# Adaptive modulation in four column strips, split over two places; memory keys and values moved to the start

## The chip, the core and the metric

The program is one kernel on one core of a Trainium2 chip. The core has five engines with a queue of instructions each: TensorE (PE; its weight loads are PEld), VectorE (DVE), ScalarE (ACT), GpSimd (POOL) and SyncE (SP, which here only issues transfers). An engine works strictly through its own queue; between engines, order is kept by semaphores that an instruction raises and another waits for. The metric is the device time of one execution in microseconds (us).

## The reference, cut to what matters

The whole computation is a hybrid mixer block, a feed-forward block and two attention or recurrent layers over 1024 tokens of width 1024. The change touches three small pieces of it: the modulation of the first block (a vector of 1024 times a matrix of 1024 x 6144, giving six vectors), the first norm that uses two of them, and the keys and values of a memory of 256 rows, which only the second block reads.

```
c_act = jax.nn.silu(c)
mod = c_act @ ada_w[l] + ada_b[l]
sh1, sc1, gt1, sh2, sc2, gt2 = [m[:, None, :] for m in jnp.split(mod, 6, axis=-1)]
h = rms_norm(x, pre1_w[l]) * (1.0 + sc1) + sh1
y = hybrid_mixer(h, w_in[l], ...)
x = x + (1.0 + gt1) * rms_norm(y, post1_w[l])
h = rms_norm(x, pre2_w[l]) * (1.0 + sc2) + sh2
...
mem_kv = (mem @ w_mem_kv[layer]).reshape(b, MEM_LEN, 2, N_MEM_HEADS, HEAD_DIM)
```

So the mixer needs `sh1` and `sc1` (a third of the matrix) before its first product; `gt1`, `sh2`, `sc2`, `gt2` are needed only when the mixer is done.

## The kernel before, in words

**Blocks.** The program is a row of blocks; all engines meet at a barrier between two of them. In a block, `side_by_side` takes several parts, and each part yields a planned time before each step on each engine; the steps are merged by these planned times, and that alone sets the order of an engine's queue. The planned times are not waits. An instruction that waits for a semaphore holds up all that stands behind it on its engine.

**Weights.** All products with large weights run in two-part precision: a weight slot is 128 x 1024 numbers (512 KB). SP fetches it into one of two raw buffers (`raw_w`), ACT rounds it (`round_slot`, L269), POOL subtracts to get the rest (`rest_of_slot`, L278, which raises `w_split`), and both halves go to a ring of four slots. PE then makes three products per weight tile (hi x hi, hi x lo, lo x hi; `three`, L286). A raw buffer is free for the next transfer when POOL is done with it; a place in the ring is free when PE is done with its slot.

**The front block** (L1212) does four things. The modulation (L967) streams 48 slots of 512 KB of `ada_w` in plain f32 through PE: the vector, repeated over 128 columns, is the stationary operand, and each slot is two products of 128 x 128 by 128 x 512 into one PSUM bank. All 128 rows of the result are the same; DVE picks the diagonal (L993, L997) for each group of four slots. `squares` loads x in four quarters and sums squares; `statistic` makes the mean and root (L819 to L851); `normed` scales x on DVE (L1074), rounds it with the shift added on ACT (L1086) and takes the rest on DVE (L1078), which gives `h_hi` and `h_lo`, the moving operand of the mixer. The memory part (L1108 to L1198) lies in x's buffer, so it starts when the norm is done; its two layers of keys and values use weight slots 0 to 7 and leave through DRAM.

**The three mixer blocks** behind it multiply h with the weight stream. The second of them (L1728) uses PSUM banks 0 to 3 for other work; the third (L1828) runs twelve products of 8 k-tiles by 1024 tokens (gate, queries, S5 inputs; banks 4 to 7 only), with a convolution on DVE beside them, and then eight products of 4 k-tiles that merge. A block that waits for the keys and values to be in DRAM (`finish(kv_written)`, L915) stands between the first and the second.

## Time and profile before

| what | value |
|---|---|
| time, median of 3 runs | 3321.97 us |
| the three runs | 3309.07, 3321.97, 3329.38 us |
| profiled execution, span | 3327.0 us |
| PE busy | 3077.8 us, 93% of the span |
| DVE, ACT, POOL busy | 39%, 29%, 24% |
| read from DRAM, written | 207.10 MB, 51.99 MB; 78 GB/s over the span |
| memory traffic in the first 105 us | 34.35 MB, mean 327 GB/s |
| first product of the mixer starts at | 139.10 us |

The profiled execution's time is known only as its span from the first to the last instruction, 3327.0 us, which lies among the three runs (0.15% above their median). In the profile, PE is busy nearly throughout, so time is lost or won where PE waits, and where it does work that could be shorter.
### The profile page before, as it was taken

To read this page: it belongs to the slowest core of one execution; us is meant where nothing else is said; L and a number is where in the kernel's file an instruction comes from. 1 tells how busy PE (TensorE), PEld (TensorE's weight loads), DVE (VectorE), ACT (ScalarE), POOL (GpSimd) and SP (SyncE) were. 2 spreads that over 40 slices of the span, in tenths; PEclk is the share of its full clock that TensorE was granted. 3 is DMA by queue.
4 is the path that set the end of the run, shared out by engine and by line. 5 is a ranking of instruction groups with operands and counts; after the bars stand their busy time and mean duration, and the time that the engine had idled before them with its cause. 6 is when DMAs were issued, how large, how long until landed. Compare 5 with 4: busy or idle time off the path is not lost. (4 is left out here: it accounts for less than half of the span.)

```text
span 3327.0 us, 33614 instructions
## 1 busy us (share of the span) xinstructions
PE 3077.8 (93%) x14024; PEld 2305.5 (69%) x14024; DVE 1302.5 (39%) x1342; ACT 977.6 (29%) x1264; POOL 809.4 (24%) x380
## 2 busy tenths in 40 slices
PE   8899999999989898999999999998789998899886
PEld 3677777877766576688888787776466666667565
DVE  5153111333425443300000245331656663528555
ACT  3232222212134123311111354332233441247312
POOL 1223112215332122322222345322021211223100
PEclk9999999999989899899999999998789999999897
DMA  9411111252132342111111233312100001111201
GB/s 355 140 52 58 57 51 57 108 177 77 64 131 92 107 172 72 55 44 50 44 44 50 75 112 123 112 51 86 57 19 15 20 14 70 64 70 38 92 13 51
DMA packets 76485, 261.01 MB, mean 78 GB/s; under 512 B 8048, under 2 KB 12384, under 8 KB 75328
## 3 DMA queue, kind: packets, MB, share of 16 engines
q1 hardware_dynamic: 76352, 259.13, 22.1%
q8 instruction: 97, 1.59, 0.2%
q14 instruction: 36, 0.29, 0.0%
HBM read 207.10 MB, written 51.99 MB: 78 GB/s over the span
## 5 line engine op out<-in xcount | busy, mean ns | idle before, releaser
L278 POOL TENSOR_TENSOR w_lo_sb<-raw_w_sb,w_hi_sb 128x1024 fp32r<-128x1024 f32 x231 | 579.5, 2509 | 2003.1 <-ACT w_hi_sb L269 2002.9
L269 ACT ACTIVATE w_hi_sb<-raw_w_sb 128x1024 fp32r<-128x1024 f32 x231 | 243.1, 1052 | 418.1 <-PE ps L286 369.0
L286 PE MATMUL ps<-merged_parts_hi_sb,w_hi_sb 128*128 128x512 f32 x832 | 336.0, 404 | 16.4 <-PEq L533 7.7
L286 PE MATMUL ps<-merged_parts_lo_sb,w_hi_sb 128*128 128x512 f32 x832 | 332.3, 399 | 0.0
L286 PE MATMUL ps<-h_hi_sb,w_hi_sb 128*128 128x512 f32 x720 | 296.4, 412 | 14.7 <-PEq L907 11.1
L286 PE MATMUL ps<-h_lo_sb,w_hi_sb 128*128 128x512 f32 x720 | 288.4, 401 | 0.0
L286 PE MATMUL ps<-merged_parts_hi_sb,w_lo_sb 128*128 128x512 f32 x832 | 274.1, 398 | 0.0
L286 PE MATMUL ps<-h_hi_sb,w_lo_sb 128*128 128x512 f32 x720 | 245.1, 400 | 0.0
L286 PE MATMUL ps<-z_lo,w_hi_sb 128*128 128x512 f32 x512 | 205.8, 402 | 0.0
L286 PEld LDWEIGHTS ps<-merged_parts_hi_sb,w_hi_sb 128*128 128x128 f32 x832 | 158.4, 190 | 61.9 <-issue 13.8
L2768 DVE TENSOR_TENSOR ffn_hidden_sb<-ffn_hidden_sb,ps 128x1024 f32 x20 | 24.4, 1221 | 426.0 <-PE ps L286 426.0
L286 PEld LDWEIGHTS ps<-merged_parts_hi_sb,w_lo_sb 128*128 128x128 f32 x832 | 158.3, 190 | 39.7
L286 PEld LDWEIGHTS ps<-merged_parts_lo_sb,w_hi_sb 128*128 128x128 f32 x832 | 158.5, 191 | 37.2 <-issue 0.5
L286 PE MATMUL ps<-z_hi,w_hi_sb 128*128 128x512 f32 x384 | 162.7, 424 | 15.9 <-POOL z_lo L3517 5.9
L286 PEld LDWEIGHTS ps<-h_hi_sb,w_hi_sb 128*128 128x128 f32 x720 | 137.9, 191 | 53.1 <-issue 18.5
L286 PEld LDWEIGHTS ps<-h_hi_sb,w_lo_sb 128*128 128x128 f32 x720 | 137.6, 191 | 34.0
L286 PEld LDWEIGHTS ps<-h_lo_sb,w_hi_sb 128*128 128x128 f32 x720 | 138.2, 192 | 32.1 <-issue 1.0
L286 PE MATMUL ps<-hid_hi_sb,w_hi_sb 128*128 128x512 f32 x352 | 141.2, 401 | 7.7 <-DVE hid_lo_sb L2863 7.7
L286 PE MATMUL ps<-hid_lo_sb,w_hi_sb 128*128 128x512 f32 x352 | 140.2, 398 | 0.0
L286 PE MATMUL ps<-hid_hi_sb,w_lo_sb 128*128 128x512 f32 x352 | 139.1, 395 | 0.0
L3225 PE MATMUL ps<-qh_sb,kh_sb 97*128 97x512 f32 (+3 forms) x288 | 125.3, 517 | 13.1 <-DMA qh_sb<-att_rows 10.5
L286 PE MATMUL ps<-z_hi,w_lo_sb 128*128 128x512 f32 x384 | 133.9, 403 | 0.0
(571 smaller groups left out, 5571.9 us busy)
## 6 DMA issues: line engine op xcount, KB each, us to landing
raw_w_sb<-in_w SPq DMA_DIRECT2D x231, 512.0 KB, 3.2
ada_w_sb<-in_ada SPq DMA_DIRECT2D x48, 512.0 KB, 7.2
inbox_sb<-gates_out SPq DMA_DIRECT2D x24, 512.0 KB, 4.1
gates_out<-outbox_sb SPq DMA_DIRECT2D x16, 512.0 KB, 2.6
inbox_sb<-sums_out SPq DMA_DIRECT2D x16, 512.0 KB, 4.7
spilled_sum<-x_sb SPq DMA_DIRECT2D x32, 256.0 KB, 2.0
x_sb<-spilled_sum SPq DMA_DIRECT2D x2, 4096.0 KB, 13.5
x_sb<-in_x SPq DMA_DIRECT2D x4, 1024.0 KB, 10.9
```

The source lines that it names most:

```text
L269: nc.scalar.activation(w_hi[:, n % RING].rearrange("p t m -> p (t m)"), raw_w[:, n % RAW], ACT.Copy).then_inc(w_rounded.sem, 1)
L278: nc.gpsimd.tensor_tensor(w_lo[:, n % RING].rearrange("p t m -> p (t m)"), raw_w[:, n % RAW], flat_hi, ALU.subtract).then_inc(w_split.sem, 1)
L286: mm = nc.tensor.matmul(o, wt, xs, start=start and part == 0 and xs is x_hi, stop=stop and part == 1)
L2768: return nc.vector.tensor_tensor(late[:, tile], late[:, tile], src, ALU.mult)
L3225: mm = nc.tensor.matmul(ps[:, 4 + n % 2, 0:hi - lo], k_of(u)[0:dq + 1, s * P:(s + 1) * P], q_of(u)[0:dq + 1, lo:hi], start=True, stop=not ...
```

## The change

1. The modulation product is cut into four column strips of 32: the stationary operand is the vector repeated over 32 columns, and the four strips of the array take four different pieces of 128 columns of the slot. The slots are laid out anew on the host side to suit. DVE picks from 128 x 128 instead of 128 x 512.
2. Only the first 16 of the 48 slots are done in the front (ring of 6 buffers instead of 8). The other 32 go into the third mixer block (`late_modulation`), one slot at each 4.2 us of planned time, with two buffers.
3. The memory keys and values come at the start of the front: their input lies where `h_lo` will be, so the first writes of `h_lo` wait until all eight steps are done (`kv_t`, 8). The raw weight transfers 2 to 13 are issued among the modulation's.
4. In the norm, half of the `h_lo` work goes from DVE to POOL, at the price of one more ACT instruction for these tiles.
5. The wait for keys and values in DRAM moves from a block of its own into SP's queue at the end of the front block.

```diff
-ADA_RING = 8
+ADA_RING = 6
 ADA_SLOTS = 48
+ADA_EARLY = 16
...
+        wide_scope = ctx.enter_context(ExitStack())
+        act0_wide = sb_in(wide_scope, "ada_silu", [P, DT, 32], high=True)
+        own_row = sb_in(wide_scope, "ada_own_row", [P, 32], high=True)
...
+        def modulate(n, slot, bank, count):
+
+            for k in range(2):
+                for s in range(4):
+                    mm = nc.tensor.matmul(ps[strip_of(s), bank, 0:P], act0_wide[:, 2 * (n % 4) + k],
+                                          slot[:, k, s * P:(s + 1) * P], start=(n % 4 == 0 and k == 0),
+                                          stop=(n % 4 == 3 and k == 1), tile_position=(0, 32 * s))
+            mm.then_inc(count.sem, 1)
+
+        def pick_group(g, pick, bank, picked, link):
+
+            nc.vector.tensor_tensor(pick, ps[:, bank, 0:P].rearrange("p (j i) -> p j i", i=32),
+                                    own_row[:].unsqueeze(1).broadcast_to([P, 4, 32]), ALU.mult).then_inc(picked[0].sem, 1)
+            link.eng.wait_ge(picked[0].sem, picked[1])
+            link(nc.vector.tensor_reduce(mod[:, 4 * g:4 * g + 4], pick, AX.X, ALU.add))
...
-            S = lambda n: 8.0 + 1.9 * n
-            X = lambda i: S(2 + 5 * i)
+            S = lambda n: 12.0 + 2.2 * n
+            X = lambda i: 4.0 + 8.0 * i
+            K = lambda n: 15.0 + 3.2 * n
+            N0 = S(ADA_EARLY) + 2.0
...
-                    for n in range(ADA_SLOTS):
+                    for n in range(ADA_EARLY):
                         yield S(n)
...
-                        for k in range(2):
-                            mm = nc.tensor.matmul(ps[:, n // 4 % 2], act0_wide[:, 2 * (n % 4) + k],
-                                                  ada_w[:, n % ADA_RING, k], start=(n % 4 == 0 and k == 0),
-                                                  stop=(n % 4 == 3 and k == 1))
-                        mm.then_inc(pe_done.sem, 1)
+                        modulate(n, ada_w[:, n % ADA_RING], n // 4 % 2, ada_done)
...
+            split_at = lambda n: 10.5 + 2.6 * n if n < RING else K(n - RING) + 4.6
+
             def first_slots():
-                at = lambda n: S(8 + 4 * (n - RAW)) if n >= RAW else -1.0 + n
-
                 def on_sp(sp):
-                    for n in range(RING + RAW):
-                        yield at(n)
+                    for n in range(RING + 8 + RAW):
+                        yield -3.0 + 0.1 * n if n < RAW else split_at(n - RAW) + 2.6
                         if n >= RAW:
                             sp.wait_ge(w_split.sem, n - RAW + 1)
                         sp.dma_start(raw_w[:, n % RAW], a["w"][n]).then_inc(w_full[n % RAW].sem, 16)
...
                 def on_dve(dve, link):
                     for t in range(10):
-                        yield A + 1.7 * t
+                        yield A + 1.2 * t
...
-                        if t >= 2:
+                        if t >= 2 and t % 2 == 0:
                             dve.wait_ge(hi_s.sem, n - 1)
+                            if n == 2:
+                                dve.wait_ge(kv_t.sem, 8)
                             nc.vector.scalar_tensor_tensor(H[1][:, t - 2, cols], x0[:, t - 2, cols], mod[:, t - 2:t - 1],
...
+                        if t % 2 == 0:
+                            nc.scalar.activation(H[0][:, t, cols], x0[:, t, cols], ACT.Identity, bias=mod[:, t:t + 1]
+                                                 ).then_inc(hi_s.sem, 1)
+                        else:
+                            nc.scalar.activation(x0[:, t, cols], x0[:, t, cols], ACT.Identity, bias=mod[:, t:t + 1]
+                                                 ).then_inc(biased_s.sem, 1)
+                            act.wait_ge(biased_s.sem, n // 2 + 1)
+                            nc.scalar.activation(H[0][:, t, cols], x0[:, t, cols], ACT.Copy).then_inc(hi_s.sem, 1)
+
+                def on_pool(pool, link):
+                    for t in range(1, 8, 2):
...
+                        pool.wait_ge(hi_s.sem, n + 1)
+                        nc.gpsimd.tensor_tensor(H[1][:, t, cols], x0[:, t, cols], H[0][:, t, cols].bitcast(F32),
+                                                ALU.subtract).then_inc(lo_pool_s.sem, 1)
...
-            memT = sb_over("mem_in", [P, DT, MEM], F32, x0_at)
...
+            memT = sb_over("mem_in", [P, DT, MEM], F32, h_lo_at)
+            MT = (sb_over("mem_parts_hi", [P, DT, MEM], F32R, h_lo_at + 8 * T),
+                  sb_over("mem_parts_lo", [P, DT, MEM], F32R, h_lo_at + 16 * T))
+            km = [sb_in(scope, f"mem_k{layer}", [65, MEM_HEADS, MEM]) for layer in range(2)]
+            vm = [sb_in(scope, f"mem_v{layer}", [P, MEM // P, MEM_HEADS, P]) for layer in range(2)]
...
             def memory_keys():
                 def on_sp(sp):
-                    yield after_norm
-                    sp.wait_ge(lo_s.sem, 16)
+                    yield -2.5
                     sp.dma_start(memT[:], a["mem"]).then_inc(mem_s.sem, 16)
...
+                    yield N0 + 20.0
+                    sp.wait_ge(kv_written.sem, 64)
 
                 def on_pe(pe):
...
-                            yield at + m * step
+                            yield K(n)
...
+        def late_modulation(scope, at, pace):
+
+            slots = sb_in(scope, "ada_late", [P, 2, 2, HALF])
...
+            n_late = ADA_SLOTS - ADA_EARLY
+            L = lambda n: at + pace * n
+
+            def on_sp(sp):
+                for n in range(n_late):
+                    yield L(n - 2) + 0.6
+                    if n >= 2:
+                        sp.wait_ge(*done.at(n - 1))
+                    sp.dma_start(slots[:, n % 2].rearrange("p k m -> p (k m)"), a["ada"][ADA_EARLY + n]
+                                 ).then_inc(full[n % 2].sem, 16)
+
+            def on_pe(pe):
+                for n in range(n_late):
+                    yield L(n)
+                    if n % 4 == 0 and n >= 8:
+                        pe.wait_ge(*picked.at(n // 4 - 1))
+                    pe.wait_ge(*full[n % 2].at(16 * (n // 2 + 1)))
+                    modulate(n, slots[:, n % 2], n // 4 % 2, done)
+
+            def on_dve(dve, link):
+                for g in range(n_late // 4):
+                    yield L(4 * g + 3) + 1.2
+                    dve.wait_ge(*done.at(4 * g + 4))
+                    pick_group(g + ADA_EARLY // 4, pick[:], g % 2, (picked, picked.n + g + 1), link)
...
-            finish(kv_written)
-            kv_scope.close()
             finish(rows_written)
...
-            side_by_side(gate, gating(), queries, convolution(), inputs, Part(None, ready), merging)
+            late = late_modulation(s2, 8.0, 4.2)
+            side_by_side(gate, gating(), queries, convolution(), inputs, Part(None, ready), merging, late)
...
+def _by_strip(slots):
+
+    n = slots.shape[0]
+    return np.ascontiguousarray(slots.reshape(n, P, 2, 4, 4, 32).transpose(0, 1, 2, 4, 3, 5)).reshape(n, P, SLOT * P)
```

**SP in the front block.** `ada_w` are the modulation's slots, `raw_w` the weight slots, `x` the quarters of the input; `pe_done` is raised by a modulation slot in the kernel before, `ada_done` in the changed one. Before, from its first wait on:

```order
L955 DMA ada_w_sb_60<-in_ada 128x1024 [waits pe_done]
L1037 DMA x_sb_57<-in_x 128x4x512
L955 DMA ada_w_sb_60<-in_ada 128x1024 [waits pe_done] x5
L1037 DMA x_sb_57<-in_x 128x4x512
L955 DMA ada_w_sb_60<-in_ada 128x1024 [waits pe_done]
L1016 DMA raw_w_sb_49<-in_w 128x1024 [waits w_split]
```

And in the changed kernel, from its first wait on:

```order
L984 DMA ada_w_sb_62<-in_ada 128x1024 [waits ada_done]
L1029 DMA raw_w_sb_49<-in_w 128x1024 [waits w_split]
L984 DMA ada_w_sb_62<-in_ada 128x1024 [waits ada_done]
L1029 DMA raw_w_sb_49<-in_w 128x1024 [waits w_split]
L984 DMA ada_w_sb_62<-in_ada 128x1024 [waits ada_done]
L1029 DMA raw_w_sb_49<-in_w 128x1024 [waits w_split]
L984 DMA ada_w_sb_62<-in_ada 128x1024 [waits ada_done]
L1050 DMA x_sb_59<-in_x 128x4x512
L1029 DMA raw_w_sb_49<-in_w 128x1024 [waits w_split]
```

Where there was a weight transfer after every fourth or so modulation slot, the two now take turns, and the third quarter of x stands behind three weight transfers that wait for POOL.

**PE in the third mixer block**, in the middle of one of its products (`h_hi`, `h_lo` times weights). Before:

```order
L286 MATMUL ps<-h_hi_sb_58,w_hi_sb_50 128x512
L286 MATMUL ps<-h_lo_sb_59,w_hi_sb_50 128x512
L286 MATMUL ps<-h_hi_sb_58,w_hi_sb_50 128x512
L286 MATMUL ps<-h_lo_sb_59,w_hi_sb_50 128x512
L286 MATMUL ps<-h_hi_sb_58,w_lo_sb_51 128x512 x2
```

Changed, with one late slot of the modulation between two k-tiles (the semaphore shown as `mem_loaded` is a used one, taken over for the late slots' landing):

```order
L287 MATMUL ps<-h_hi_sb_60,w_hi_sb_50 128x512
L287 MATMUL ps<-h_lo_sb_61,w_hi_sb_50 128x512
L287 MATMUL ps<-h_hi_sb_60,w_lo_sb_51 128x512 x2
L939 MATMUL ps<-ada_late_sb_3361,ada_silu_sb_57 32x128 [waits mem_loaded]
L939 MATMUL ps<-ada_late_sb_3361,ada_silu_sb_57 32x128 x7
L287 MATMUL ps<-h_hi_sb_60,w_hi_sb_50 128x512
L287 MATMUL ps<-h_lo_sb_61,w_hi_sb_50 128x512
```

There are 32 such places, each of eight short products, each with its own wait for a transfer.

**SP in the third mixer block**, of the changed kernel: the late slots' transfers stand among waits for POOL (`w_split`) and for ACT (`ml_silu`). Their wait (shown as `mem_lo`, also a used semaphore) is for the late slot two before.

```order
L1249 DMA ada_late_sb_3361<-in_ada 128x1024 [waits mem_lo] x3
L589 DMA raw_w_sb_49<-in_w 128x1024 [waits w_split]
L1249 DMA ada_late_sb_3361<-in_ada 128x1024 [waits mem_lo]
L1851 DMA ml_qk_out<-conv_box_sb_3343 128x1024 [waits ml_silu]
L1249 DMA ada_late_sb_3361<-in_ada 128x1024 [waits mem_lo]
```

In the kernel before, the same stretch holds the `raw_w` and `ml_qk_out` transfers alone.

## Rows read from the trace of the kernel before

**Rows 1.** Stretches: us, busy us (records) by engine, granted clock, DMA share, GB/s
```profile
0.00:20.00 20.00, 12.72 (x23) 5.57 (x24) 2.07 (x3) 3.61 (x4) 4.86 (x6) 1.00 0.92 352
20.00:60.00 40.00, 35.84 (x84) 16.34 (x82) 22.14 (x34) 15.63 (x24) 4.70 (x2) 0.91 1.03 398
...
105.00:128.00 23.00, 23.00 (x193) 22.73 (x191) 3.02 (x11) 9.39 (x15) 12.07 (x6) 1.00 0.38 131
128.00:139.10 11.10, 0.01 (x1) 0.03 (x1) 0.88 (x4) 2.11 (x2) 6.92 (x3) 0.71 0.69 226
533.00:712.00 179.00, 178.68 (x761) 143.32 (x759) 49.42 (x32) 38.90 (x35) 41.45 (x16) 0.99 0.34 115
```

**Rows 2.** Timeline of PE in the front: start, length, engine, line, operation, count
```profile
69.01 36.21 PE L967 MATMUL ps<-ada_w_sb,ada_silu_sb 128*128 128x512 f32 x84
104.66 0.68 PE L286 MATMUL ps<-mem_parts_hi_sb,w_hi_sb 128*128 128x256 f32 x1
...
127.72 0.28 PE L286 MATMUL ps<-w_hi_sb,mem_parts_lo 128*128 128x256 f32 x1
139.10 0.76 PE L286 MATMUL ps<-h_hi_sb,w_hi_sb 128*128 128x512 f32 x1 [11.10 <-PEq L907]
```

**Rows 3.** Timeline of POOL, last row of the front
```profile
134.72 2.34 POOL L278 TENSOR_TENSOR w_lo_sb<-raw_w_sb,w_hi_sb 128x1024 fp32r<-128x1024 f32 x1 [1.42 <-ACT w_hi_sb L269]
```

**Rows 4.** Timeline of SP and ACT: first quarter of x issued, and first used
```profile
11.43 0.43 SPq L1037 DMA_DIRECT2D x_sb<-in_x  x1
...
22.71 0.63 ACT L1049 ACTIVATE norm_total_sb<-x_sb 128x512 f32<-128x512 f32 x1 [9.34 <-DMA x_sb<-in_x]
```

**Rows 5.** Transfers of the page, whole span: KB each, median us to landing
```profile
raw_w_sb<-in_w SPq DMA_DIRECT2D x231, 512.0 KB, 3.2
```

**Rows 6.** Groups by line, page: busy us, mean ns of one
```profile
L278 POOL TENSOR_TENSOR w_lo_sb<-raw_w_sb,w_hi_sb 128x1024 fp32r<-128x1024 f32 x231 | 579.5, 2509 | 2003.1 <-ACT w_hi_sb L269 2002.9
L269 ACT ACTIVATE w_hi_sb<-raw_w_sb 128x1024 fp32r<-128x1024 f32 x231 | 243.1, 1052 | 418.1 <-PE ps L286 369.0
```

**Rows 7.** Timeline of DVE in the first norm
```profile
76.34 0.74 DVE L1078 SCALAR_TENSOR_TENSOR h_lo_sb<-x_sb,mod_sb,h_hi_sb 128x512 fp32r<-128x512 f32 x1
77.01 0.74 DVE L1074 SCALAR_TENSOR_TENSOR x_sb<-x_sb,fold_sb,ps 128x512 f32<-128x512 f32 x1
77.67 0.74 DVE L1078 SCALAR_TENSOR_TENSOR h_lo_sb<-x_sb,mod_sb,h_hi_sb 128x512 fp32r<-128x512 f32 x1
```

**Rows 8.** Timeline of ACT: two with a bias back to back, two without
```profile
73.16 1.38 ACT L1086 ACTIVATE h_hi_sb<-x_sb,mod_sb 128x512 fp32r<-128x512 f32 x2 [2.43 <-DVE x_sb L1074]
...
23.25 1.13 ACT L1049 ACTIVATE norm_sq_sb<-x_sb 128x512 f32<-128x512 f32 x2
```

**Rows 9.** Groups of POOL by shape: half-width subtractions elsewhere
```profile
L3517 POOL TENSOR_TENSOR z_lo<-x_sb,z_hi 128x512 fp32r<-128x512 f32 x8 | 10.8, 1346 | 42.7 <-ACT z_hi L3511 42.7
```

**Rows 10.** Timeline of PE: column strips of 32 inside a stream of two-part products
```profile
809.83 0.39 PE L286 MATMUL ps<-h_lo_sb,w_hi_sb 128*128 128x512 f32 x1
810.06 0.40 PE L286 MATMUL ps<-h_hi_sb,w_lo_sb 128*128 128x512 f32 x1
810.39 3.70 PE L1944 MATMUL ps<-s_state_sb,s_c_powers_sb 128*32 128x128 f32 x128
814.02 0.50 PE L286 MATMUL ps<-h_hi_sb,w_hi_sb 128*128 128x512 f32 x1
814.35 0.40 PE L286 MATMUL ps<-h_lo_sb,w_hi_sb 128*128 128x512 f32 x1
```

**Rows 11.** Timeline of PE: sixteen records in strips, twice as wide
```profile
787.44 1.07 PE L1926 MATMUL ps<-s_c_powers_sb,s_bbar_sb 128*32 128x256 f32 x16 [1.12 <-POOL act_sb L2005]
788.45 0.50 PE L286 MATMUL ps<-h_hi_sb,w_hi_sb 128*128 128x512 f32 x1
```

**Rows 12.** Waits of PE from 128 to 800 us: total, times, longest
```profile
PE ps L286 <- PEq L915: 2.9, 1, 2.9
...
PE ps L286 <- PEq L1268: 2.5, 1, 2.5
```

**Rows 13.** Groups of DVE by line, 533 to 712 us
```profile
L1792 DVE SCALAR_TENSOR_TENSOR conv_box_sb<-ml_raw_sb,vec_sb,conv_box_sb 128x1024 f32<-128x1024 f32 x12 | 23.5, 1960 | 0.4
```

**Rows 14.** Timeline of SP in the third mixer block: transfers in regular steps
```profile
597.50 0.33 SPq L1808 DMA_DIRECT2D ml_qk_out<-conv_box_sb  x1
605.20 0.33 SPq L588 DMA_DIRECT2D raw_w_sb<-in_w  x1
608.69 0.33 SPq L1808 DMA_DIRECT2D ml_qk_out<-conv_box_sb  x1
```

154 lines of the change are left out of this document (69 added, 85 removed).

## The prediction

> **What bounds the kernel now.** I read the stretches first. From 0 to 60 us two things are full at once: PE, nearly all of it modulation, and the memory traffic at about 400 GB/s; the granted clock is near 1. From 105 to 128 us PE works on keys and values while memory is at 131 GB/s, and from 128 to 139 us PE does nothing. From 533 to 712 us, in the third mixer block, PE is busy 178.68 of 179 us [rows 1]. So the front leaves PE's main work, the two-part products, unstarted for 139.10 us [rows 2], and everything behind it is bound by PE: what is put into the third block is paid in full, what is taken from the front is gained in full as long as nothing else there takes its place.
>
> The timeline of PE then gives the prices. 84 modulation records take 36.21 us, 0.43 us each, four to a slot: 1.72 us, against 512 KB / 0.405 MB/us = 1.3 us of transfer. Keys and values are 192 products from 104.66 to 128.0 us, 2.9 us for each of eight weight slots [rows 2]. The idle 11 us are the weight pipeline: POOL's last split ends at 137.06 [rows 3], the barrier follows, and PE starts 2.0 us later [rows 2].
>
> **The front, step by step.** Removed from PE: 32 slots x 1.72 = 55 us. The remaining 16 slots cost 0.78 us each as strips (next part): 12 us. Keys and values stay 8 x 2.9 = 23 us but lie beside the transfers. PE therefore needs some 35 us at full clock, POOL 12 splits x 2.5 = 30 us [rows 6], so neither alone is the bound.
>
> Transfers: they land in the order of issue. The first quarter of x was issued at 11.43 with 7.6 MB up to its end, and was used at 22.71 [rows 4]: that is 4 us + 7.6 MB / 0.405. The changed order has, up to the last of the 16 slots, 26 transfers of 0.52 MB, x with 4.2, the memory rows with 1.05, constants 0.75, stored keys and values 0.8: 20.4 MB, so 54 us if SP never had to hold. It does hold. There are two raw buffers, and SP issues raw slot n+2 only after split n; landing 3.2 us at least [rows 5], rounding 1.05, split 2.5 [rows 6]: 6.8 us for each pair, plus 1.3 us for every other slot that lies ahead of it in the transfers. Walking the new order of SP, ACT, POOL and PE with these durations I get: split 0 at 14 us (ACT first waits for the memory rows), raw 3 issued at 21, raw 4 at 30, the third quarter of x landed at 37, the fourth at 50, raw 9 landed at 57, modulation slot 15 at 59. PE in its strict order does the last value step until 62, then the sums of the fourth quarter, then the last strips until 67; picking, bias and fold on DVE end at 69. The bounds of this point: 59, if the holds cost nothing (54 and the last strips and picks), and 88, if TensorE runs the whole front at 1.2 GHz, so that each key step takes 5.7 us and PE's own queue is the chain.
>
> The norm follows whole, because the scaling of both halves stands behind the second root on DVE. DVE steps are 0.66 us apart [rows 7]. Of each two tiles DVE now does three operations (1.98 us); ACT does a biased rounding and a biased write (two back to back take 1.38) and a copy (0.57, half of 1.13) [rows 8], with a semaphore between, some 2.04 us. Eight such pairs: 16.3 us; the first scaling 0.7; behind the last rounding one POOL subtraction of half width, 1.35 us [rows 9]. Together 18.4 us, so the block ends at 87.5 to 88 and the mixer's first product starts at 90 (2.0 us of barrier as before). **Gain 49 us**; with the bounds of the fold, 60 and 30.
>
> **The price of a late slot.** The trace holds this very instruction elsewhere: 128 x 32 stationary, 128 x 128 moving, four strips in turn [rows 10]. From the product at 810.06 to the one at 814.35 pass 4.29 us; two ordinary steps of 0.23 are in it, so 128 records with their change of mode cost 3.82. Sixteen records of twice the width take 1.01 us up to the next product [rows 11], without the 0.10 us lag on entry (810.39 - 810.06 - 0.23) and the 0.10 after the first product (814.35 - 814.02 - 0.23). With g for a group of four records and o for entry and exit: 32 g + o = 3.82 and 8 g + o - 0.20 = 1.01, so g = 0.109 us and o = 0.34. The four strips do overlap. A slot is sixteen records: 4 x 0.109 + 0.34 = 0.78 us, and **32 late slots cost 25 us**, all on PE's path. Bounds: 14 us (no o), and 67 us (records one after another, 16 x 0.109 + 0.34).
>
> The Trainium skill has two rules against this part. "TensorEngine Tiling (Array Packing)", Key Properties, says that changing the tiling mode drains TensorE; o is what the trace shows of it. "TensorE: Matmul & The Clock Gate", in the section on 56 ns, gives an issue bound of about 62 ns per matmul when the decoding is not done in hardware; by it a slot would be 16 x 62 ns + 0.34 = 1.33 us and the late part 43 us. The trace disagrees, 27 ns per record [rows 10].
>
> **The rest of the third block.** Late transfers are 16.8 MB in about 200 us and fit beside 115 GB/s [rows 1]. A slot's transfer is issued when the slot two before is done, some 10 us ahead of its use, and lands in 3.2 us [rows 5]; SP's regular steps there show it not holding long for others [rows 14]. The picks add eight pairs of small operations to DVE, which is busy 49 of 179 us [rows 1], with its convolution at 2 us an operation [rows 13]. The banks used (0, 1) are free. I cost all this at nothing; if the cover of 10 us went, each slot would cost PE up to its landing. The removed barrier block: three meetings took 2.9 us of PE and two took 2.5 [rows 12]; I take 1 us.
>
> **The sum.** -49 - 1 + 25 = -25 us: 3302 against the profiled 3327.0, and 3297 against the median 3322, which lies 5 us below the profiled span. About 1%, 33 us, is what a measurement here can tell from no change.
>
> **Rivals.**
> - *TensorE cold in the front* (12%). For it: its clock fell in the stretches with idle PE (0.71 from 128 to 139 us [rows 1]), and the new front has waits for splits of up to 6 us between its pieces. Against: the old front with its gaps stayed at 0.91 [rows 1]. Fold at 88, product at 109: -30 - 1 + 25, time 3316.
> - *A shorter front* (10%). Transfers hold SP less than my walk says; fold near 60: -59 - 1 + 25, time 3287.
> - *Issue-bound strips* (3%). If short bursts cost by the record and not by the group of four, the dearest step that a row shows is 1.01 / 16 = 0.063 us [rows 11]; a slot is then 16 x 0.063 + 0.34 = 1.35 us and the late part 43 us, time 3315. Against: the long burst [rows 10]. The Trainium skill's issue bound, above, is this rival.
> - *Strips that do not overlap here* (3%), the change not doing what it says: 67 us instead of 25, and some 10 us more in the front, time 3349. Rows 10 speak plainly against.
> - *Starved late slots, slower than before* (4%). SP's queue is strict: 18 of the 32 late transfers stand directly behind a wait for POOL, ACT or an outbox. If SP gets there only after the slot is due, PE stands for the landing, 3.2 us: 18 x 3.2 = 58, time 3355. It decides from a mean wait of 0.8 us per late slot. Against it, the 10 us of cover and the regular steps [rows 14].
>
> The forecast of 3297 keeps 68%; its own range is 3284 to 3310. The range for 8 in 10 takes in the colder and the shorter front, and half a run-to-run spread (3309 to 3329 before): 3278 to 3319. Faster by over 1% (below 3289): most of the shorter front and a fifth of the forecast, 22%. Slower by over 1% (above 3355): half of the last two rivals, 5%. Within 1%: 73%.
>
> **What would show it.** In the changed profile: the first `h_hi` product at 90 us (right from 82 to 98); modulation slots in the front waiting for transfers or splits, not PE being full; strips of sixteen records taking 0.44 us with gaps of about 0.1 on both sides; PE without waits for `ada_late` in the third block, which grows from 179 to about 204 us; DVE and ACT working alone for 18 us before the mixer. Wrong would be a front product later than 100 us, PE waits on late transfers, or a change in any block that the diff does not touch.

## The result, and the profile after

The changed kernel takes 3297.02 us (median of 7 runs, 3294.3 to 3306.13) against 3322.66 us for the kernel before (7 runs, 3309.07 to 3329.38): a ratio of 0.993, 95% interval [0.991, 0.995]. The forecast was 3297. That agreement is closer than the working deserves: the front gained 7 us less than forecast, and stretches at a lower clock in blocks that the change does not touch gave back about as much. The profile shows both.

Stretches of the changed kernel first: us, busy us (records) of PE, PEld, DVE, ACT, POOL, then TensorE's granted clock, DMA share, GB/s. The first four are the front, the last is the third mixer block; they answer to [rows 1].

```profile
0.00:20.00 20.00, 6.47 (x53) 5.35 (x53) 9.86 (x16) 7.61 (x15) 4.02 (x6) 1.00 0.92 353
20.00:60.00 40.00, 29.57 (x317) 26.42 (x317) 15.06 (x22) 16.76 (x26) 16.37 (x8) 0.87 0.84 309
60.00:76.30 16.30, 9.56 (x107) 7.70 (x98) 9.89 (x19) 5.66 (x9) 8.36 (x4) 0.69 0.54 187
76.30:96.75 20.45, 0.90 (x2) 0.03 (x1) 17.20 (x24) 15.74 (x24) 10.17 (x8) 0.50 0.12 46
...
482.00:685.00 203.00, 202.47 (x1273) 152.19 (x1271) 54.92 (x52) 38.89 (x35) 38.62 (x16) 1.00 0.56 182
```

The front is now 97 us long instead of 139, and its last 20 us are the norm on DVE, ACT and POOL alone. The third block has grown from 179 to 203 us and PE stands in it for only 0.5 us, with 182 GB/s of traffic beside it instead of 115.

PE's timeline in the front, the first statistic and then the end (start, length, engine, line, operation, count, idle time before and its releaser), for [rows 2]:

```profile
40.84 1.87 PE L820 MATMUL ps<-cst_sb,norm_total_sb 128*128 128x1 f32 x8 [6.99 <-DVE norm_total_sb L1072]
...
69.81 1.87 PE L820 MATMUL ps<-cst_sb,norm_total_sb 128*128 128x1 f32 x8 [6.00 <-DVE norm_total_sb L1072]
71.61 2.79 PE L939 MATMUL ps<-ada_w_sb,ada_silu_sb 128*32 128x128 f32 x48
75.13 2.07 PE L827 MATMUL ps<-norm_diag_sb,cst_sb 128*128 128x512 f32 x2 [0.73 <-DVE norm_diag_sb L831]
96.75 0.77 PE L287 MATMUL ps<-h_hi_sb,w_hi_sb 128*128 128x512 f32 x1 [19.55 <-PEq L908]
```

The mixer's first product starts at 96.75 us where the prediction had 90. Ahead of it PE stood 6 us for the sums of the fourth quarter of x, and then did the last three strip slots behind them.

PE's timeline in the third block, two of the late slots between ordinary products, for [rows 10, 11]:

```profile
493.27 0.63 PE L287 MATMUL ps<-h_hi_sb,w_lo_sb 128*128 128x512 f32 x2
493.83 0.64 PE L939 MATMUL ps<-ada_late_sb,ada_silu_sb 128*32 128x128 f32 x16
494.40 0.50 PE L287 MATMUL ps<-h_hi_sb,w_hi_sb 128*128 128x512 f32 x1
...
498.24 0.63 PE L287 MATMUL ps<-h_hi_sb,w_lo_sb 128*128 128x512 f32 x2
498.80 0.64 PE L939 MATMUL ps<-ada_late_sb,ada_silu_sb 128*32 128x128 f32 x16
```

From one late slot to the next are 4.97 us with eighteen products of 0.233 us in between (4.20 us), so a slot costs 0.77 us; the forecast was 0.78.

To see where time came and went, take the same instruction in two traces. The lead of a kernel over the changed one is the time of an instruction in the changed kernel's trace minus its time in the other; the head row gives the first. A kernel whose lead jumps between two columns gained or lost there.

```
instruction at (us)     132    263    310    424    492    684   1108   2059   3281
kernel before         -42.5  -44.9  -48.7  -52.0  -51.2  -27.2  -26.8  -31.4  -31.5
c1 (changed, again)    -0.3   -0.3   -0.2   -0.3   -0.3   -0.3   -0.1   -0.2   +0.8
e2 block put back      -0.6   -3.0   -7.0  -10.2  -10.3  -10.2   -8.0   -7.5   -7.7
e4 x earlier           +2.6   +2.2   +2.3   +2.2   +2.2   +2.2   +4.0   +2.2   +8.6
e7 pairs               -1.0   -3.2   -4.4   -7.6   -8.1   -2.2   -2.1   -7.0   -8.0
e1b no late slots      -1.0   -3.2   -4.4   -7.7   -6.9  +17.1  +14.6   +9.9  +15.5
e8 order              +12.8  +10.5   +9.4   +6.2   +6.1   +6.1   +8.6   +9.2   +9.2
e9 order and pairs    +12.6  +12.2  +12.3  +12.3  +11.8  +17.7  +18.2  +16.0  +23.5
e5 all in front       -47.4  -49.0  -48.5  -48.6  -47.8  -23.8  -25.7  -30.4  -31.4
e5b same, early fold  -26.7  -29.0  -29.8  -33.0  -32.2   -8.2  -13.1  -15.9  -13.7
e6 two strips          +0.4   +0.0   +0.1   +0.1   +0.0   +0.5   +2.8   +3.4   +4.3
e10 keys last         -18.3  -19.9  -20.2  -21.8  -20.3  -20.3  -20.5  -25.4  -25.4
e3 norm on DVE         -4.8   -6.4   -6.3   -8.0   -6.4   -6.4   -7.0   -8.9   -2.8
```

Read the first line so: the front gained 42.5 us, block 3 (492 to 684) gave back 24.0 (51.2 to 27.2), and 9.5 us were gained between 132 and 424 us, in blocks of which the diff touches only the removed barrier block. Where these 9.5 us come from, the same piece of the program shows, from the instruction at 132 to that at 424, in the kernel before and in the changed one:

```profile
174.72:476.07 301.35, 290.83 (x1646) 232.02 (x1645) 91.98 (x116) 85.67 (x77) 68.44 (x47) 0.95 0.14 51
```
```profile
132.25:424.14 291.89, 281.77 (x1647) 224.66 (x1645) 91.96 (x116) 85.79 (x77) 68.41 (x47) 0.98 0.15 53
```

It is the same work on every engine, but PE was busy 9.1 us longer with it, at a granted clock of 0.95 instead of 0.98, and idle 0.4 us longer (10.5 against 10.1).

### The profile page after: what moved, and what is told of

It is laid out like the page before. It is cut to its first block and busy times, and to the rows that moved or that the text cites. A ratio compares the mean times of both kernels' runs of the same rounds, so it can differ in the third digit from the quotient of the medians.

```text
span 3295.5 us, 34766 instructions
## 1 busy us (share of the span) xinstructions
PE 3021.5 (92%) x14600; PEld 2278.5 (69%) x14600; DVE 1297.3 (39%) x1335; ACT 981.6 (30%) x1272; POOL 817.5 (25%) x388
```

## The experiments

### The late slots: e1b, e6, e7

**e1b_no_late**: the late part without its transfers, strips and picks.

```diff
-            part = Part(on_sp, on_pe, None, on_dve)
+            part = Part(None, None, None, on_dve)
...
+                link(nc.vector.memset(mod[:, 16:48], 0.0))
```

> The changed kernel with its late slots left out of the third mixer block (their transfers, strips and picks); the last 32 columns of the modulation before the bias are set to zero instead. Theory: the 32 slots cost 25 us of TensorE's path and nothing else, so 3297 - 25 = 3272 us, block 3 back at 179 us, no other block moved. Rival 1: they also slow what is beside them or later blocks (transfers, clock), then 3264 or less. Rival 2: part of the late work fills time that was idle anyway, then 3280 or more.

Measured: 3276.04 us (3269.07 to 3286.51), ratio to before 0.9856 [0.9833, 0.988]; 21 us below the changed kernel's 3297. In the trace, where the rest of the program can't blur it, the block is 24.0 us shorter (lead -6.9 to +17.1). The theory stands for the block: 24 us, all on PE's path. Behind it the lead wanders (14.6, 9.9, 15.5), as it does in runs whose program differs from the changed kernel's in nothing there (e2, e4).

**e6_two_strips**: half of each late slot's records left out.

```diff
-                for s in range(4):
+                for s in range(strips):
...
+                    modulate(n, slots[:, n % 2], n // 4 % 2, done, strips=2)
```

> The changed kernel with two of the four column strips left out in the late slots alone (half of each late slot's products; the other half of the values stays what an earlier use of the bank left). Theory: the four strips run at the same time, a slot costs 4 groups x 0.109 us + 0.34 us whether a group has two records or four; the step between products stays at 0.77 us and the time at 3297 us. Rival: records cost 27 ns each in turn; then 8 fewer records save 0.22 us a slot, step 0.55 us, 7 us in all: 3290 us.

Measured: 3295.15 us (3292.95 to 3296.73). PE's timeline in the third block:

```profile
493.20 0.63 PE L287 MATMUL ps<-h_hi_sb,w_lo_sb 128*128 128x512 f32 x2
493.76 0.63 PE L939 MATMUL ps<-ada_late_sb,ada_silu_sb 128*32 128x128 f32 x8
494.32 0.50 PE L287 MATMUL ps<-h_hi_sb,w_hi_sb 128*128 128x512 f32 x1
...
498.17 0.63 PE L287 MATMUL ps<-h_hi_sb,w_lo_sb 128*128 128x512 f32 x2
498.72 0.63 PE L939 MATMUL ps<-ada_late_sb,ada_silu_sb 128*32 128x128 f32 x8
```

Eight records take the time of sixteen: 0.63 us against 0.64, the step 4.96 against 4.97, the lead over the block 0.0 to +0.5. So the third and fourth strip of a group cost nothing beside the first two; e7 below shows that groups do cost. The Trainium skill, "TensorE: Matmul & The Clock Gate", in its section on 56 ns, gives an issue bound of about 62 ns per matmul without decoding in hardware; by an estimate from it, eight records fewer would have saved 0.5 us a slot, and the trace shows 0.01.

**e7_pairs**: two late slots back to back, both buffers refilled behind them.

```diff
-                    yield L(n - 2) + 0.6
+                    yield L(n - n % 2 - 2) + 2.0
                     if n >= 2:
-                        sp.wait_ge(*done.at(n - 1))
+                        sp.wait_ge(*done.at(n - n % 2))
...
-                    yield L(n)
+                    yield L(n - n % 2)
```

> The changed kernel with the late slots taken two at a time (a pair of slots back to back every 8.4 us of planned time, both buffers refilled behind the pair). Theory: each entry and exit of the strips costs 0.34 us, so 16 fewer of them save 5.4 us: 3291.5 us, 32 records take about 1.2 us from product to product. The refill has 8 us for two transfers of 3.2 us and stays hidden. Rival 1: the cost is by record, not by entry, so nothing changes (3297). Rival 2: the refill comes late, behind other waits of SP, and PE waits for slots: 3300 or more.

Measured: 3300.18 us (3291.58 to 3305.28), where the theory had 3291.5: no gain. Yet its trace has the pairs as the theory says, and the third block 5.9 us shorter (lead -8.1 to -2.2):

```profile
496.44 1.08 PE L939 MATMUL ps<-ada_late_sb,ada_silu_sb 128*32 128x128 f32 x32
497.45 0.50 PE L287 MATMUL ps<-h_hi_sb,w_hi_sb 128*128 128x512 f32 x1
```

32 records to the next product: 1.01 us, against twice 0.57, and the lags of 0.1 us on either side once instead of twice. PE has no wait for a slot in the block, so rival 2 is out although its time came true. In the trace the gain is hidden because this execution lost 6.6 us between 132 and 424 us, before the first late slot, to stretches at the lower clock. The other runs did too, it seems: the mean granted clock over the span was 0.943 to 0.945 in six of seven, and 0.946 or more in six of seven of the changed kernel. Whether that is chance or comes with the pairs stays open in this run; e9 answers it for its own front.

### The blocks behind the front: e2, c1

**e2_block_back**: the empty block for the keys and values again.

```diff
+            finish(kv_written)
             finish(rows_written)
```

> The changed kernel with the empty block for the keys and values put back between the first and the second mixer block. Theory A: the block costs about 1 us, and the 9.5 us that the trace of the change gained between 232 and 480 us are half-clock stretches of TensorE that fall differently from execution to execution: time 3298 us, and the stretches before block 3 fall anywhere. Rival B: the block itself costs 4 us or more (the lead over the kernel before went from 44.9 to 48.7 us across it): time 3301 us or more, and the lead falls back by 3.8 us at the line behind the block.

Measured: 3300.56 us (12 runs, 3291.63 to 3314.36), some 3 us above the changed kernel. Product before the boundary, and the one after it, in e2:

```profile
296.29 0.63 PE L287 MATMUL ps<-h_hi_sb,w_lo_sb 128*128 128x512 f32 x2
300.17 0.77 PE L287 MATMUL ps<-w_hi_sb,h_hi_sb 128*128 128x512 f32 x1 [3.25 <-PEq L916]
```

and in e7, which has no such block:

```profile
295.06 0.63 PE L287 MATMUL ps<-h_hi_sb,w_lo_sb 128*128 128x512 f32 x2
298.54 0.47 PE L287 MATMUL ps<-w_hi_sb,h_hi_sb 128*128 128x512 f32 x1 [2.86 <-PEq L916]
```

The block itself costs 0.4 us of idle time (3.25 against 2.86), and the first product behind it takes 0.77 us instead of 0.47: PE comes back at the lower clock. From 263 to 310 us e2 falls behind by 4.0 us in all, e7 and e1b by 1.2. But most of that is lost before the boundary is reached. The 8 us that start at 266 us, PE's columns as above, in e2 and then in e7:

```profile
266.00:274.00 8.00, 8.00 (x27) 6.26 (x26) 1.35 (x2) 0.00 (x0) 0.00 (x0) 0.65 0.00 0
```
```profile
266.00:274.00 8.00, 8.00 (x34) 6.40 (x33) 1.36 (x2) 0.68 (x1) 0.00 (x0) 0.83 0.00 0
```

Of the 4.0 us, 2.6 lie ahead of the boundary, where PE had not reached the block yet; 0.4 are the wait, and 1.0 is the lower clock behind it. So by these traces the block costs 0.4 us, and 1.4 us at most. e10 below has the block too, waits 3.26 us at it, and falls behind by only 0.3 us over the same stretch. Theory A was right about the price; its time of 3298 and B's 3301 can't be told apart (the ratio's interval is 13 us wide). B's fall of the lead came true, but the block's own wait and the clock behind it make only 1.4 us of it. The kernel before, with the block too, loses 2.7 us more than the changed one ahead of the boundary; why the clock is low there is open.

**c1_after_again**: the changed kernel, unchanged.

> The changed kernel once more, as a control for the clock. Theory: the blocks behind the front hold short half-clock stretches at the same places in every execution (behind the block changes at about 255, 300, 410 and 485 us), whose length differs from execution to execution; so leads against other kernels change at these places alone, and the time is 3297 us, within 5 us. Rival: the first trace shows what this kernel always does; then the new trace agrees with it to 1 us at every line.

Measured: 3297.82 us (3295.36 to 3306.45). The rival won: its trace agrees with the first to 0.3 us up to 2059 us. Stretches of 20 us, about the same piece of the program in four traces (first mixer block): the kernel before, the changed kernel, c1, e7.

```profile
298.00:318.00 20.00, 19.11 (x102) 15.84 (x103) 2.68 (x4) 1.54 (x2) 2.15 (x4) 0.66 0.08 27
```
```profile
253.00:273.00 20.00, 18.17 (x125) 14.76 (x124) 2.72 (x4) 2.67 (x3) 7.08 (x6) 1.00 0.20 79
```
```profile
253.00:273.00 20.00, 18.17 (x125) 14.72 (x124) 2.73 (x4) 2.96 (x3) 6.79 (x6) 1.00 0.21 79
```
```profile
254.00:274.00 20.00, 18.17 (x105) 14.81 (x104) 2.69 (x4) 0.68 (x1) 4.58 (x5) 0.74 0.11 38
```

The third number from the right is the granted clock. PE is busy 18.2 to 19.1 us in all four, but in the kernel before it ran here at 0.66 and in e7 at 0.74. So there are two patterns: in one the blocks at 263, 310 and 424 us hold long half-clock stretches (before, e2, e7, e1b, e8, e5b), in the other short or none (changed, c1, e4, e5, e6, e9; e3 and e10 lie close to it). Measured as PE's busy time from 132 to 424 us, with the same products, it is 281.7 to 281.8 us in the short pattern, 283.3 in e3 and e10, 288.1 in e7, e1b, e8 and e5b, and 290.6 and 290.8 in e2 and the kernel before. The changed kernel got the short one in both its traces, the kernel before the long one in its only trace. e7, e1b and e2 are the changed kernel up to here, but for what lies later or in one empty block, and got the long one, so the front alone does not fix it. What picks the pattern stays open.

### The front: e4, e8, e10, e5, e5b, e3

**e4_x_early**: third and fourth quarter of x issued earlier.

```diff
-            X = lambda i: 4.0 + 8.0 * i
+            X = lambda i: (4.0, 12.0, 16.5, 21.0)[i]
...
-                        yield X(i)
+                        yield (4.0, 12.0, 16.5, 17.0)[i]
```

> The changed kernel with the third and fourth quarters of x issued together behind weight transfer 3 (planned 16.5 and 17.0 instead of 20 and 28), and the squares of the fourth quarter planned at 21 instead of 28. Theory: what put the fold at 76 us instead of 69 is the fourth quarter of x, issued at 48 us, and its squares behind the rounding of slot 9; early, the second statistic leaves the chain, the fold comes at 62 to 66 us, the mixer's first product at 84 to 88 us instead of 96.75, time 3297 - 10 = 3287 us. Rival: POOL's splits and TensorE's strict order hold the last strips anyway, the first product stays at 95 +- 2 us and the time at 3296.

Measured: 3297.28 us (3288.68 to 3308.25), first product at 93.76 us: 3.0 us instead of 9 to 13. PE's timeline says why:

```profile
44.38 1.87 PE L820 MATMUL ps<-cst_sb,norm_total_sb 128*128 128x1 f32 x8 [9.33 <-DVE norm_total_sb L1072]
...
60.17 1.05 PE L820 MATMUL ps<-cst_sb,norm_total_sb 128*128 128x1 f32 x8
...
68.91 1.13 PE L827 MATMUL ps<-norm_diag_sb,cst_sb 128*128 128x512 f32 x2 [0.51 <-DVE norm_diag_sb L831]
69.96 1.96 PE L939 MATMUL ps<-ada_w_sb,ada_silu_sb 128*32 128x128 f32 x64
```

The second statistic no longer waits (60.17), but the first, which already held PE for 6.99 us in the changed kernel, now stands at 44.38 in front of key steps and holds it for 9.33 us, and the last four strip slots stand behind the second diagonal. The cause was right, the cure moved the wait: an early step in a strict queue delays all that stands behind it.

**e8_order**: all planned times of the front set so that no queue's head comes late, and a ring of 8.

```diff
-            S = lambda n: 12.0 + 2.2 * n
-            X = lambda i: 4.0 + 8.0 * i
-            K = lambda n: 15.0 + 3.2 * n
+            S = lambda n: 11.1 + 2.1 * n
+            X = lambda i: (8.4, 13.8, 19.4, 24.0)[i]
+            K = lambda n: 14.6 + 3.1 * n
...
-                        yield S(n - ADA_RING) + 1.0
+                        yield -1.0 + 0.1 * n if n < 2 else 4.4 + 2.15 * n
...
-                        yield X(i)
+                        yield (0.0, 17.5, 21.2, 27.2)[i]
...
-                at = X(2 * h + 1) + 12.0
+                at = (27.8, 37.4)[h]
```

> The changed kernel with other planned times in the front alone, and a ring of 8 modulation buffers: weight transfers 2 and 3 ahead of modulation slots 5 to 7, the second to fourth quarters of x spread between weight transfers, both statistics late (planned 27.8 and 37.4). e4 took the fourth quarter of x out of the chain and won 3 us of 10, because the first statistic then held TensorE's queue and the key steps behind it. Theory: the front is set by the order of the strict queues; with every queue's head ready in time the fold comes at 58 to 65 us, the mixer's first product at 78 to 86 us instead of 96.75, time 3297 - 10 to 18 = 3279 to 3287 us. Rival: the weight pipeline (two raw buffers, POOL) or slow DVE sums beside POOL hold it; first product at 90 us or later, time 3292 or more.

Measured: 3285.32 us (3280.74 to 3290.36), ratio to before 0.9881 [0.9862, 0.99]. Fold at 62.86, first product at 83.82. The same instructions in another order, with two more buffers, gain 12.9 us: not the work set the changed kernel's front, but the order of the queues and the size of the ring. The two were changed together, so their shares are not known. PE now has no wait of 7 us for the first statistic (1.8 at 38.52), and the last modulation slot lands 4 us earlier, at 60.5. Traffic in e8's middle stretch is 338 GB/s at a share of 0.92, against 309 at 0.84 from 20 to 60 us in the changed kernel:

```profile
20.00:62.90 42.90, 36.05 (x411) 30.76 (x406) 28.93 (x38) 23.39 (x37) 21.89 (x9) 0.89 0.92 338
```

**e10_keys_last**: the kernel before with strips and split alone (keys and values, norm, empty block as they were). Its diff is that of the change without the parts on `memory_keys`, `first_slots`, `normed` and X; S, and the ring of 8, stay as before.

```diff
-                    for n in range(ADA_SLOTS):
+                    for n in range(ADA_EARLY):
...
+                        modulate(n, ada_w[:, n % ADA_RING], n // 4 % 2, pe_done)
...
+            late = late_modulation(s2, 8.0, 4.2)
```

> The kernel before with the column strips and the split of the modulation alone (16 slots in front, 32 in the third block); keys and values behind the norm, DVE's norm, the empty block, x and weight transfers where they were. Theory: the split alone takes the transfers and TensorE's work away, but keys and values still follow the norm: fold near 48 us, norm done at 70, memory rows and their rounding 7.5 us, eight steps of 2.9, the pipeline's 11 and the barrier's 2: first product near 113 us (105 to 118) instead of 96.75; time 3297 + 16 = 3313 us. Rival: the early keys bring nothing of their own (the weight pipeline bounds both), then the first product stays below 100 us and the time at 3300.

Measured: 3315.38 us (12 runs, 3304.48 to 3322.78), ratio to before 0.9966 [0.9949, 0.9983]; first product at 114.06 us. The theory had 113 and 3313, so the rival is out. The norm is done on DVE at 71.9, and key steps still follow it. The first product is 17.3 us later than in the changed kernel and the time 18 us longer. POOL's share of the norm (2.4, e3 below) is part of the 17.3; the removed block (0.4, e2) lies behind it. So early keys with their order of transfers are worth some 15 us.

**e5_all_front** and **e5b_front_early_fold**: all 48 slots as strips in the front, none late; in e5 the fold for the norm comes behind the 48th slot, in e5b behind the 16th.

```diff
-ADA_EARLY = 16
+ADA_EARLY = 48
...
-            side_by_side(gate, gating(), queries, convolution(), inputs, Part(None, ready), merging, late)
+            side_by_side(gate, gating(), queries, convolution(), inputs, Part(None, ready), merging)
```

and in e5b besides

```diff
+                        if g == 3:
+                            link(nc.vector.tensor_tensor(mod[:, 0:16], mod[:, 0:16], V("ada_b", 0, 16), ALU.add))
+                            folded([(0, ("pre1_w", 8))], link)
```

> The changed kernel with all 48 slots as strips in the front, none late. Theory: what made the front short is that 32 transfers (16.8 MB) left it; with them back the front is bound by transfers, 37 MB at 0.405 MB/us = 92 us and the last strips and picks, and SP's holds on top: fold near 105 to 115 us, first product at 125 to 135 us. The late part's 25 us are gone, so 3297 + 33 - 25 = about 3305 us. Rival: the strips alone were the gain (they took 40 us of PE's work out) and the split adds nothing: first product below 120 us, time 3290 or less.

> e5 again (all 48 slots as strips in the front, none late), but with the fold of the first norm behind the 16th slot, as in the kernel before, and not behind the 48th. In e5 the norm's 19 us stood behind the last slot, first product at 144.2 us, and 32 slots took 1.28 us each, which is one slot's transfer. Theory: the norm now hides beside the slots, the first product comes at 126 to 129 us, and against the changed kernel the time is +31 - 24 = +7: 3304 us. So of the front's gain the strips and early keys are 10 to 13 us, the moving of slots 30. Rival: another 19 us are not hidden, since DVE, ACT and PE hold each other up, first product at 135 us or later.

Measured: e5 3327.21 us (10 runs, 3316.68 to 3330.77), ratio to before 1.0001 [0.9988, 1.0015], first product at 143.18; e5b 3299.77 us (4 runs, 3295.01 to 3310.98), ratio 0.9925 [0.9897, 0.9954], first product at 123.14. The fold in e5 came at 122 us and the norm's 19 us behind all slots, where the expectation had 105 to 115, and the time is 22 us above the 3305 expected; since the kernel before folds behind slot 16, e5 does not price the split. e5b does; its first product comes 3 us before the 126 to 129 expected, so its rival is out. PE in e5, where only slots stream:

```profile
97.28 1.08 PE L939 MATMUL ps<-ada_w_sb,ada_silu_sb 128*32 128x128 f32 x16 [0.21 <-DMA ada_w_sb<-in_ada]
98.56 1.08 PE L939 MATMUL ps<-ada_w_sb,ada_silu_sb 128*32 128x128 f32 x16 [0.20 <-DMA ada_w_sb<-in_ada]
```

One slot each 1.28 us, released by its transfer: 32 slots more are 41 us of transfers, of which the norm in e5b covers a part. The split gains 26.4 us of front (123.14 - 96.75) and costs 24.0 in block 3, so by the trace it is worth 2.4 us. By the times it is 2 to 3 us, which four runs that spread over 16 us can't tell from nothing. Both kernels have the queue order that e8 improved; what the split is worth with a better order in front was not tried.

**e3_norm_dve**: the first norm on DVE and ACT alone, as before.

```diff
-                        if t >= 2 and t % 2 == 0:
+                        if t >= 2:
...
-                return Part(None, None, on_act, on_dve, on_pool)
+                return Part(None, None, on_act, on_dve)
```

> The changed kernel with the first norm as before: all sixteen h_lo subtractions on DVE, none on POOL, one ACT rounding per tile. Theory: DVE's 32 operations then set the norm, 32 x 0.66 = 21.1 us and one more rounding and subtraction behind the last scaling, 22.5 us instead of 18.8; first product at 100.5 us instead of 96.75, time 3297.5 + 3.7 = 3301 us, which in time alone can hardly be told from no change. Rival: in the changed kernel DVE works beside POOL and is slowed there; without POOL's part it is faster than the sum says, and the first product stays within 1 us of 96.75.

Measured: 3298.33 us (3292.68 to 3304.2), which can't be told from the changed kernel. In the trace the first product is at 100.68, as forecast; but 1.5 us of the delay are there at the fold already (77.37 against 75.84), so POOL's share of the norm is worth 2.4 us from fold to product (23.3 against 20.9), not 3.7.

### A better version: e9

**e9_order_pairs**: e8's order of the front and e7's pairs; its diff is theirs.

> e8's front and e7's pairs of late slots together. e8 gave 3285.3 us. Theory: in its trace e7 shortened block 3 by 5.9 us (32 records from product to product in 1.01 us instead of two steps of 0.57 and the 0.1 us lags), which its own time did not show because the half-clock stretches around it were long. Together 3285.3 - 5.5 = 3280 us, the block 24 - 5.5 = 18 to 19 us longer than without late slots. Rival: what pairs save in block 3 is given back by the clock behind it, time 3285 us as e8.

Measured: 3274.61 us (6 runs, 3265.24 to 3277.57), ratio to before 0.985 [0.9827, 0.9874]. All of its runs lie below all of c1's on the same chip (3295.36 to 3306.45). First product at 83.69, third block 5.9 us shorter than the changed kernel's, both as the theory has it; the time is 5 us better than its 3280. In the traces, e9 is 11.6 us ahead of e8 at 684 us, and 5.9 of them are the pairs: the rest is that e9 has the short pattern of half-clock stretches and e8 the long one. So pairs do not always bring the long one, and about half of that lead over e8 is clock, not design.

## Why the prediction came out right, step by step

**Late part, 25 us: right.** 24.0 by the leads, 24.0 by e1b; 0.77 us a slot against 0.78. The two terms of the price were tested apart: the overlap by e6 (records left out cost nothing), the entry and exit by e7 (16 fewer of them gain 5.9 us where 16 x 0.34 = 5.4). The transfers stayed hidden: PE stands 0.5 us in 203. The rivals of issue-bound, non-overlapping and starved slots are out. The Trainium skill, "TensorEngine Tiling (Array Packing)", Key Properties, says that changing the mode drains TensorE; the trace agrees, with the 0.34 us.

**Norm and barrier: right.** Forecast 18.4 us from the fold to the last subtraction, measured 18.8 (76.41 to 95.2), then 1.5 us to the first product instead of 2.0.

**The front's gain of 49 us: 7 us too large.** The step that failed is the walk up to the fold: its end was forecast for 69 us and came at 76.0. It held for what SP issues up to 30 us (raw 3 at 20.9 for 21, raw 4 at 30.2 for 30) and for the last value step of PE (63 for 62), but not for the landings behind that. The fourth quarter of x landed at 54.6 us for 50, raw 9 at 63.3 for 57, and modulation slot 15 at 64.6 for 59 (issued at 48.05, 53.89 and 56.26, and landing 6.5, 9.4 and 8.3 us later). So 6 of the 7 us were lost before the end of the chain began. Two things stand out in the trace. PE waited 6.99 us for the first statistic; behind it a key step and slot 6 came late, and only then could SP issue slot 12 (47.68) and the fourth quarter. And the stored keys and values, issued at 53.06 and 53.49, lie ahead of raw 9: from slot 14's landing to raw 9's pass 4.0 us where one slot takes 1.3. That the order and the ring are the cause, and not the work, e8 shows by getting 12.9 us back; which of the two things above weighs more was not tried apart.

From raw 9's landing to the end of the fold the walk had 12 us and the trace has 12.7, though three terms in it were not at their undisturbed length. First, ACT's queue: the squares of the fourth quarter, whose input had landed, stand behind the rounding of slot 9, which waited for its transfer.

```profile
63.34 1.06 ACT L270 ACTIVATE w_hi_sb<-raw_w_sb 128x1024 fp32r<-128x1024 f32 x1 [3.66 <-DMA raw_w_sb<-in_w]
64.31 1.13 ACT L1062 ACTIVATE norm_sq_sb<-x_sb 128x512 f32<-128x512 f32 x2
```

Second, DVE beside POOL. Timelines of DVE and POOL in the changed kernel, and then of both in e4:

```profile
64.95 4.81 DVE L1072 TENSOR_TENSOR norm_total_sb<-norm_total_sb,norm_sq_sb 128x512 f32<-128x512 f32 x4 [12.34 <-ACT norm_sq_sb L1062]
72.36 2.71 DVE L831 TENSOR_TENSOR norm_diag_sb<-cst_sb,norm_stat_sb 128x512 f32<-128x512 f32 x1
```
```profile
69.85 4.67 POOL L279 TENSOR_TENSOR w_lo_sb<-raw_w_sb,w_hi_sb 128x1024 fp32r<-128x1024 f32 x2 [3.03 <-ACT w_hi_sb L270]
```
```profile
51.38 0.69 DVE L831 TENSOR_TENSOR norm_diag_sb<-cst_sb,norm_stat_sb 128x512 f32<-128x512 f32 x1
```
```profile
52.25 2.40 POOL L279 TENSOR_TENSOR w_lo_sb<-raw_w_sb,w_hi_sb 128x1024 fp32r<-128x1024 f32 x1 [2.34 <-ACT w_hi_sb L270]
```

The same diagonal takes 0.69 us while POOL is idle (51.38, POOL starts at 52.25) and 2.71 us while POOL subtracts (72.36, beside 69.85 to 74.52). Not all of that is on the path: the last strips end at 74.4 and the last pick starts at 75.00, so the slow diagonal delays the fold by 0.6 us. The first of the four sums, which takes 2.42 us beside POOL where the others take 0.69, holds up the chain of squares and sums by 1.7. Third, TensorE's clock, at 0.69 from 60 to 76 us: the three strip slots took 2.79 us where 3 x 0.78 was forecast, a small part. The rival of a cold front was thus right in kind and small in size.

**The removed block, 1 us: right within what the runs can tell.** It is 0.4 us of waiting and up to 1.0 us of lower clock behind it (e2), 0.4 with e10.

**What made the sum come out.** Front +42.4, block +0.4, late part -24.0: about 19 us of gain. The medians differ by 25.6 us (17 to 30 by the interval of the ratio), the traces by 31.5. In the traces 9.1 us of the rest are shown to be clock: PE was that much longer busy with the same work between 132 and 424 us; most of what is left lies behind block 3 and was not looked into. This is a sign that the prediction had named against itself, a change in blocks that the diff does not touch. For the medians, the 7 us between 19 and 25.6 can only be argued to be the same, since each kernel's runs spread over 10 us and more. So the mechanism and the late part's price were right and the walk was not; that the time hit the forecast to the microsecond is luck, since the front's missing 7 us were made up by a clock that nobody had forecast. One sum of the prediction is also off by itself: half of the last two rivals' 7% is 3.5%, not the 5% given for slower by over 1%.

**Where the change's gain is.** Of its parts, early keys bring some 15 us (e10), POOL's share of the norm 2.4 (e3), the removed block 0.4 to 1.4 (e2), the split 2.4 (e5b, by one trace). Strips by themselves, without early keys or the split, were not tried. What carries the title, a late third block for two thirds of the modulation, is worth next to nothing once strips have made a slot cheap for PE: a slot late costs 0.77 us of PE, and in front it costs a transfer of 1.28 us, of which part is covered (26.4 us for 32 slots in e5b, 0.83 each).

## What to carry to other kernels

Price a moved piece by the resource that is full where it lands, and ask what the same piece would cost if it stayed: here the move of 32 slots was nearly an even trade, and putting an independent chain of work beside a stream was the gain. In queues that run in a strict order, a time for every instruction is not enough; look for instructions whose input comes late and see what stands behind them, since moving one early can hold more than it frees (e4), and a careful order of the same work, with two more buffers, was worth half as much again as the change (e8). Compare landings with a walk, not only issues: here the issues held until 30 us and the landings were 5 to 6 us late. A difference of a few us in one trace can be the clock; read it by leads at matching instructions, block by block, and look whether the loss lies behind the thing that is blamed or ahead of it (e2), before giving it to a cause.

## What the runs showed of the hardware

- A DVE operation that reads two operands from SBUF is slowed about fourfold beside POOL, 0.69 to 2.7 us. The norm's scalings (L1087), which read one operand from PSUM, are not. DVE and then POOL of the changed kernel:

```profile
83.93 1.25 DVE L1093 SCALAR_TENSOR_TENSOR h_lo_sb<-x_sb,mod_sb,h_hi_sb 128x512 fp32r<-128x512 f32 x1
85.10 2.05 DVE L1087 SCALAR_TENSOR_TENSOR x_sb<-x_sb,fold_sb,ps 128x512 f32<-128x512 f32 x3
87.08 0.74 DVE L1093 SCALAR_TENSOR_TENSOR h_lo_sb<-x_sb,mod_sb,h_hi_sb 128x512 fp32r<-128x512 f32 x1
```
```profile
83.36 1.27 POOL L1118 TENSOR_TENSOR h_lo_sb<-x_sb,h_hi_sb 128x512 fp32r<-128x512 f32 x1 [0.80 <-ACT h_hi_sb L1109]
85.34 1.27 POOL L1118 TENSOR_TENSOR h_lo_sb<-x_sb,h_hi_sb 128x512 fp32r<-128x512 f32 x1 [0.71 <-ACT h_hi_sb L1109]
```

  L1093 takes 1.25 us beside POOL and 0.74 alone; three of L1087 take 0.68 each, POOL or not. The Trainium skill, "GPSIMD Engine Reference", Specifications, says that POOL's interfaces to SBUF are shared with VectorE and contended by instructions with two SBUF inputs; the trace agrees. The kernel before had it too (its DVE, two of the sums of squares below, 2.42 against 0.68 us), and the prediction left it out.

```profile
36.19 2.42 DVE L1059 TENSOR_TENSOR norm_total_sb<-norm_total_sb,norm_sq_sb 128x512 f32<-128x512 f32 x1
...
56.38 0.68 DVE L1059 TENSOR_TENSOR norm_total_sb<-norm_total_sb,norm_sq_sb 128x512 f32<-128x512 f32 x1
```

- A stream of short column-strip products kept PE busy 28.56 of 36 us and was granted 0.50 all that time, where the full-width products of the kernel before, busy 35.84 of 40 us, kept 0.91 [rows 1]. Whether the narrow products or the shorter busy time brought the clock down was not tried apart. e5's row, PE's columns as above:

```profile
84.00:120.00 36.00, 28.56 (x427) 16.23 (x431) 3.47 (x12) 0.00 (x0) 0.00 (x0) 0.50 0.95 379
```

- Behind a block change TensorE can come back at the lower clock though it was busy before: the first product takes 0.77 us instead of 0.47 behind waits of 3.25 and 3.26 us (e2, e10), but also 0.76 behind one of 2.91 us (the kernel before), and 0.47 behind one of 2.86 us (e7).
